# Head of a decoder block: two adaLN vectors summed by TensorE in one-column products instead of by VectorE

## What is computed

```python
mod = jax.nn.silu(c) @ w_ada[layer] + b_ada[layer]
sh_a, sc_a, gt_a, sh_f, sc_f, gt_f = jnp.split(mod, N_MOD, axis=-1)
h = modulate(rms_norm(x, g_attn[layer]), sh_a, sc_a)   # norm * (1 + sc_a) + sh_a
proj = h @ w_in[layer]
```

## Time and profile before

| what | value |
|---|---|
| median of 3 runs | 626.9 us (625.57 to 629.08) |
| the profiled execution | 627.78 us, span of its instructions 625.8 us |
| around the span | 2.0 us |
| TensorE busy | 546.5 us (87%) |
| VectorE busy | 294.6 us (47%) |
| ScalarE busy | 184.0 us (29%) |
| GpSimd busy | 79.0 us (13%) |
| chain that ended last | TensorE 61%, VectorE 13%, DMA 13%, SyncE's queue 7% |

### The profile page before, as it was taken

The page is one execution under the profiler, slowest core; times in us unless marked ns, Lnnn a source line. Parts: engine busy times, 40 slices in busy tenths (PEclk is TensorE's granted clock), DMA queues, the critical chain, the costliest instruction groups (busy, mean ns, idle before and its releaser), DMA issues.

```text
span 625.8 us, 7694 instructions
## 1 busy us (share of the span) xinstructions
PE 546.5 (87%) x2982; PEld 343.9 (55%) x2982; DVE 294.6 (47%) x497; ACT 184.0 (29%) x328; POOL 79.0 (13%) x100
## 2 busy tenths in 40 slices
PE   1499999999978999999999747899999889879797
PEld 1377768778766676665446414445555444434443
DVE  4978673376798636562032284323322222312216
ACT  5265462344444457882042211000000000000002
POOL 8131100000010000000031111111221111110000
PEclk9999999999998999999999958999999999989999
DMA  8986855595262064001930485999999999999957
GB/s 336 398 262 232 308 193 205 172 366 202 68 214 90 2 264 206 1 1 51 426 128 34 186 339 177 407 417 421 422 420 419 419 421 420 421 420 420 410 233 293
DMA packets 42626, 169.28 MB, mean 271 GB/s; under 512 B 7848, under 2 KB 9896, under 8 KB 30308
## 3 DMA queue, kind: packets, MB, share of 16 engines
q1 hardware_dynamic: 32356, 140.81, 56.3%
q0 software_dynamic: 9104, 25.95, 11.8%
q10 hardware_dynamic: 1136, 2.11, 0.9%
HBM read 160.74 MB, written 16.25 MB: 283 GB/s over the span
## 4 chain that ended last, share of the span: by engine, by line
PE 61%; DVE 13%; DMA 13%; SPq 7%; ACT 4%; issue 2%; POOL 0%; DVEq 0%; ACTq 0%; POOLq 0%
PE banks L1784 11%; PE banks L1675 9%; PE banks L1804 5%; DMA qkT<-in_w_dram 5%; DMA obuf<-in_w_dram 4%; PE banks L1627 4%; PE banks L1510 4%; PE banks L1512 4%; PE banks L1511 4%; DVE mixT L893 3%; PE banks L1611 2%; DMA qkT<-in_w_ada_dram 2%; PE banks L1504 2%; PE banks L1502 2%; PE banks L1503 2%
## 5 line engine op out<-in xcount | busy, mean ns | idle before, releaser
L1804 PE MATMUL banks<-stage,work 128*64 128x512 f32 x168 | 60.1, 610 | 6.4 <-ACT work L855 6.4
L853 ACT ACTIVATE work<-banks 128x256 f32<-128x256 f32 x16 | 6.1, 383 | 200.3 <-PE banks L1784 200.3
L1784 PE MATMUL banks<-qkT,work 128*64 128x256 f32 x272 | 62.4, 386 | 0.0
L1675 PE MATMUL banks<-stage,mixT 128*128 128x512 f32 x128 | 56.2, 595 | 0.0
L1324 DVE TENSOR_TENSOR work<-banks,gates 128x1024 f32<-128x1024 f32 x15 | 18.4, 1225 | 74.5 <-PE banks L1804 74.5
L1318 DVE TENSOR_TENSOR work<-work,banks 128x256 f32<-128x256 f32 x16 | 6.7, 421 | 87.6 <-ACT work L853 87.6
L1784 PE MATMUL banks<-hT,work 128*64 128x256 f32 x192 | 44.0, 387 | 2.5 <-DMA qkT<-in_w_dram 2.5
L1512 PE MATMUL banks<-hT_hi,w_lo 128*128 128x512 f32 x112 | 43.8, 391 | 0.0
L893 DVE SCALAR_TENSOR_TENSOR mixT<-stage,small,mixT 128x1024 f32<-128x1024 f32 x32 | 41.0, 1282 | 0.7
L1510 PE MATMUL banks<-hT_hi,w_hi 128*128 128x512 f32 x96 | 40.4, 421 | 0.0
L1675 PEld LDWEIGHTS banks<-stage,mixT 128*128 128x128 f32 x128 | 24.1, 191 | 28.8 <-issue 28.8
(11 more groups left out here) (301 smaller groups left out, 1172.6 us busy)
## 6 DMA issues: line engine op xcount, KB each, us to landing
stage<-in_w_dram SPq DMA_DIRECT2D x31, 1024.0 KB
qkT<-in_w_dram SPq DMA_DIRECT2D x23, 1024.0 KB
stage<-in_w_ada_dram POOLq DMA_DIRECT2D x16, 1024.0 KB, 5.7
hT<-in_w_dram SPq DMA_DIRECT2D x12, 1024.0 KB
stage<-in_w_in_dram SPq DMA_DIRECT2D x5, 2048.0 KB, 11.0
val<-in_w_dram SPq DMA_DIRECT2D x10, 1024.0 KB
mixT<-in_w_dram SPq DMA_DIRECT2D x10, 1024.0 KB
alibi<-in_w_dram SPq DMA_DIRECT2D x5, 1024.0 KB
```

What stands on the lines that cost most here:

```text
L1675: ins = mm(banks[:, w % 5, :], mixT[:, k, t * P:(t + 1) * P], wv[:, k % 4, half * 512:(half + 1) * 512], start=(k == 0), stop=(k == KD - 1))
L1784: ins = mm(banks[half * C:(half + 1) * C, 2, up * F:(up + 1) * F], heT[:, r, k * P + half * C:k * P + (half + 1) * C], ws[2 * place + half ...
L1804: ins = mm(banks[half * C:(half + 1) * C, 4 + 2 * r + col, :], geT[:, fc * P + half * C:fc * P + (half + 1) * C], w2s[2 * place + half][:, ...
```

## The change

VectorE's sums of the two vectors go. TensorE takes the raw weights as the stationary operand, in 128 x 128 blocks with a stride of eight elements, and the column `cs[:, r]` as the moving one, and adds up over the eight rows r in PSUM. A quarter has two rows, so it is 16 products (`column_quarter`), and there are eight quarters. Behind each of the first three quarters come the transposes of a tile of `x`, and the last tile is loaded ahead of the last two quarters and transposed ahead of the last one. Eight bf16 products of 256 columns whose result nothing reads (`HEAD_FILLERS`) stand ahead of the last quarter. In the split of `w_in`, ScalarE no longer rounds the second chunk of weights; VectorE does, behind the first part of `hT_hi`.

```diff
             for i in range(4):
+                if i == 2:
+                    x_tile(NT - 1)
                 ada_quarter(scale_w, SCALE_A, i)
-            x_tile(NT - 1)
...
             w_round(0)
-            w_round(1)
...
             dve.wait_ge(silu_c, 1)
-            first_sums(0, shift_w, shift_used)
-            first_sums(1, scale_w, scale_used)
...
             def w_rest(n):
-                raw, hi, lo, _, _ = split_chunk(n)
-                dve.wait_ge(w_hi_ready, n + 1)
+                raw, hi, lo, arrived, value = split_chunk(n)
+                if n == 1:
+                    dve.wait_ge(arrived, value)
+                    v.tensor_copy(hi, raw).then_inc(w_hi_second, 1)
+                    dve.wait_ge(w_hi_second, 1)
+                else:
+                    dve.wait_ge(w_hi_ready, max(n, 1))
                 v.tensor_tensor(lo, raw, hi.bitcast(F32), ALU.subtract).then_inc(w_split, 1)
-            w_rest(0)
             dve.wait_ge(mod_params_in, 32)
-            dve.wait_ge(col_a, 1)
+            dve.wait_ge(scale_used, KD)
...
             dve.wait_ge(mod_a, 1)
-            w_rest(1)
+            w_rest(0)
             for k in range(KD):
                 dve.wait_ge(hT_raw, k + 1)
                 v.tensor_copy(hT_hi[:, k, :], hT[:, k, :]).then_inc(hT_hi_ready, 1)
+                if k == 0:
+                    w_rest(1)
...
-            def column_sums(v, used):
-
-                pe.wait_ge(used, KD)
-                for k in range(KD):
-                    ins = mm(banks[:, 0, 8 * v + k:8 * v + k + 1],
-                             by_col[:, v, k * P:(k + 1) * P], ones[:, 0:1],
-                             start=(v + k == 0), stop=True, skip_group_check=True)
-                return ins
...
+            def column_quarter(v, i):
+
+                w, used = ((shift_w, shift_used), (scale_w, scale_used))[v]
+                pe.wait_ge(first_in[4 * v + i], 16)
+                for r in range(2 * i, 2 * i + 2):
+                    src = w[r // 4][:, r % 4, :].rearrange("p (j k) -> p k j", k=KD)
+                    for k in range(KD):
+                        ins = mm(banks[:, 0, 8 * v + k:8 * v + k + 1], src[:, k, :], cs[:, r:r + 1],
+                                 start=(v + r + k == 0), stop=(r == KD - 1), skip_group_check=True)
+                    ins.then_inc(used, 1)
+
+            pe.wait_ge(silu_c, 1)
+            for i in range(4):
+                column_quarter(0, i)
+                if i < NT - 1:
+                    x_tile_T(i)
+            for i in range(3):
+                column_quarter(1, i)
+            x_tile_T(NT - 1)
+            for n in range(HEAD_FILLERS):
+                mm(banks[:, 0, 256:512], ones_bf[:], ones_bf[:].unsqueeze(1).to_broadcast([P, 2, P]),
+                   start=False, stop=True, skip_group_check=True)
+            column_quarter(1, 3)
             pe.wait_ge(hT_raw, 1)
```

More of the change, by code:

```diff
@@ L48 @@
 FILLERS = 14
+HEAD_FILLERS = 8
 XT_BANK = (2, 3, 4, 5, 6, 7, 1, 2)
@@ L271, in hymba_block @@
         silu_c, shift_used, ada_used = sem("silu_c"), sem("shift_used"), sem("ada_used")
-        col_a, mod_a = sem("col_a"), sem("mod_a")
+        mod_a = sem("mod_a")
         xn_ready, xT_done = sem("xn_ready"), sem("xT_done")
         hT_raw, hT_hi_ready, hT_lo_dve, hT_lo_pool = (sem(n) for n in ("hT_raw", "hT_hi_ready", "hT_lo_dve", "hT_lo_pool"))
-        w_hi_ready, w_split = sem("w_hi_ready"), sem("w_split")
+        w_hi_ready, w_hi_second, w_split = sem("w_hi_ready"), sem("w_hi_second"), sem("w_split")
         job_done = sem("job_done")
@@ L901, in last_by_col @@
                                               in1=turned(sums), op0=ALU.mult, op1=ALU.add)
-            def first_sums(v, w, used):
-                for k in range(KD):
[L906 to L912, removed]
             v.memset(eps, EPS).then_inc(eps_ready, 1)
@@ L1429, in x_T, with x_tile_T @@
                                            xn[:, t, :].rearrange("p (j k) -> p k j", k=KD)[:, k, :], ident)
-            def column_sums(v, used):
-                pe.wait_ge(used, KD)
-                for k in range(KD):
-                    ins = mm(banks[:, 0, 8 * v + k:8 * v + k + 1],
-                             by_col[:, v, k * P:(k + 1) * P], ones[:, 0:1],
-                             start=(v + k == 0), stop=True, skip_group_check=True)
-                return ins
[L1440 to L1443, removed]
+            def x_tile_T(t):
                 pe.wait_ge(xn_ready, t + 1)
```

## The result

| | before | changed |
|---|---|---|
| median of 4 runs | 626.28 us | 666.27 us (664.98 to 666.4) |
| ratio on record | | 1.0631, 95% interval 1.0608 to 1.0654 |
| profiled execution, its span | 627.78, 625.8 us | 666.28, 664.2 us |
| vectors ready, ScalarE released | 36.8 us | 75.0 us |
| end of the first pair's products | 51.6 us | 90.9 us |

The kernel is 40.0 us slower by the medians and 38.5 by the two profiled executions. The head accounts for all of it: at the end of the first pair the changed kernel is 39.3 us behind, and the projection of the attention output starts 38.2 us later (324.2 against 286.0), from where the distance stays within a microsecond until the end.

The account below looks back on a forecast made before the run. VectorE's sums, not loads, were taken to hold the head; TensorE's lower-clock products would replace them. Vectors +33.1 and 1.6 behind give +34.7 on 627.8, or 662.5; 661.6 us for a median, range 646 to 672.

Parts of the forecast that it names:

- The count and the place: Head, TensorE: 128 products, 256 records at two weight loads per product, behind the loads from the first quarter on.
- The order of the loads: Head: loading x's last tile ahead of two quarters costs and gains nothing, since TensorE is behind the loads.
- Stride: Raw-block weight loads on TensorE: stride of eight taken to add nothing; upper bound 11.3 us (44 ns on each of 256 records).
- my 69.3: Head: time in us at which sums up to the vectors end at the lower clock, against 36.25 before, +33.1.
- Strided weight loads are dearer: Rival for TensorE's raw-block products: all 44 ns come on top of every record, 673 us; chance 0.05.
- My sign for it: Profile sign of dearer strided loads: weight loads of the raw-weight product group showing more than 350 ns.
- Which clock: TensorE in the head: lower clock level taken for all eight quarters, deciding between 28 and 55 us of products.
- an early rise: Rival for the head: one quarter at the lower clock, seven at the higher, +6.8 us, 633.7; chance 0.10.
- My two prices for the two levels: Head's sixteen product groups on TensorE: 54.9 us at the lower clock, 28.3 at the higher.
- Behind the vectors: From ScalarE's release to the first pair's end: 1.6 us more, between 1.0 and 2.6, from VectorE's new work and a later clock rise.
- The six `hT_lo` that end the first pair start 1.0 later: VectorE behind the vectors: 2.1 us of new rounding and `w_lo`, of which waiting absorbs 1.1.
- No loss: Rival: TensorE keeps up with the loads at 97 ns a record, 624.6 us at full success; chance 0.05.

Follow-up runs that it names:

- The run at 142 us: Kernel before, with the one-column products of the third and fourth vector reading blocks at a stride of eight: eight products took 3.67 us against 1.77.
- both runs that have this part: The changed kernel, and the kernel before with only the reordered weight split: the first pair ends 15.9 and 16.6 us behind ScalarE's release, against 14.8 before.
- the strided run: Changed kernel with twenty bf16 products of 512 columns ahead of the first quarter, blocks still strided: quarter 7.42 us, vectors at 77.8 us.

## Why the prediction was right, and where it was not

**The count and the place: right.** 256 records on TensorE in a line without gaps, behind the loads from the first quarter on, VectorE idle until the vectors come, the transposes at 1.53 for a set (1.55 written), the fillers at 1.71 (1.7). So the cause that I gave, two full weight loads for every single column, was the right one. The order of the loads cost and gained nothing: the only wait for a load was the first.

**The pace: too low by 9%.** The step was "*Stride*: I take nothing and keep 11.3 as the upper bound". Measured: 7.45 us for a quarter instead of 6.86, 0.59 x 8 = 4.7 us, of the 5.1 by which the vectors were later than my 69.3. (Most of the rest is in the three quarters without transposes between them, 22.8 us together; no run says why.) I had argued from the duration of a weight load, where 189 ns for strided transposes and 192 for unstrided products looked like one ceiling. The run at 142 us shows that the stride has a pace of its own for float32 products, which a load's duration at the lower clock (335 against 334) does not betray. So my rival "Strided weight loads are dearer", at 0.05, came true in part: 19 of its 44 ns a record. My sign for it, loads of more than 350 ns, would have missed it, for they show 335. The measured 666.3 lies just above my own spread of 657 to 666 and within the range because that reaches up for a part of the stride.

**Which clock: the granted level as predicted, but it decided nothing.** I wrote "This decides between 28 and 55 us" and gave an early rise 0.10 at 633.7. That rival rested on contiguous rows. With the blocks as the change reads them, 7.42 us for a quarter begun at 1.00, so the products would have taken about the same time. My two prices for the two levels held only for contiguous blocks. What I said for the lower level, that this kind of work had not raised the clock from 32.66 to 38.8, is borne out more strongly than I knew: it lets a clock that is up fall, with both PE and PEld at 1.00 busy in the window. The Trainium skill (TensorE: Matmul & The Clock Gate, "What's actually happening") ties the level to activity; in these windows it fell although PE and PEld read busy throughout, so by the profile's busy time alone the rule would have misled here.
The same page's section "LDWEIGHTS (loading the stationary operand)" makes the load's time a matter of its column count alone; its formula gives 107 ns for 128, an estimate. The distance between contiguous records at the higher clock comes near it (1.77 / 16 = 111 ns, though the record of the load itself is 192 ns there). The contiguous ones at the lower clock, 3.43 / 16 = 214 ns, and the strided ones at the higher, 3.67 / 16 = 229, do not.

**Behind the vectors: 1.1 to 1.8 where 1.6 was forecast, partly for the wrong reason.** The wrong step is "The six `hT_lo` that end the first pair start 1.0 later". They started no later at all, 5.84 us behind the release as before: I took 2.1 us for the new work and 0.45 for a cast without a wait, and it was 1.9 (76.49 to 78.35) and 0.37 (2.58 / 7). In both runs that have this part TensorE did not wait for them; it was late from its own stop behind the first `hT_hi` and from the lower clock, which I had priced at 0.6. That the sum came out near is in part luck.

**No loss: rightly small.** I had set its point at 97 ns a record. The strided pace is 2.4 times that.

**Profiled against profiled**: 33.1 written for the vectors, 38.2 measured; 1.6 written behind, 1.1 measured; and 0.9 gained back later in the kernel (39.3 at the end of the pair, 38.4 in the spans), which I did not follow further.

## What to carry to other kernels

A product with one moving column costs a whole 128 x 128 weight load, twice in float32, so ask for each sum which operand should be stationary: the same sums took 7.4 us a quarter with the matrix stationary (6.7 contiguous, 3.5 at the higher clock) and 1.9 at the higher clock with the vector stationary. Read a stationary operand contiguously, and take a pace from a row with the same stride and the same kind of instruction: the strided transposes said nothing of the strided products. Before counting on a higher clock, look for a row that shows the very instruction following it.

## What the runs showed of the hardware that I had not expected

- Float32 one-column products whose stationary block has a stride of eight elements run at 0.229 to 0.233 us a record at either clock level; contiguous 0.109 to 0.111 at the higher and 0.209 to 0.214 at the lower; a stride of two 0.116 at the higher. Transposes at a stride of eight follow the clock, seven in 0.84 and 1.53 us.
- The granted clock fell from 1.00 to 0.5 while TensorE's matmuls and weight loads were busy for 1.00 of the window, with products of one column, strided (from 9.72 us on) or contiguous (from 10.23 on, with seven transposes among them).
- The column of the granted clock can't be trusted before its first fall. It reads 1.00 through all of the changed kernel's head, whose transposes run at the lower pace. Among the twenty fillers of the strided run, durations went from 634 to 379 ns near 7.2 us with no change in that column, so durations have to be read before it.
- Thirty-two records with 64 stationary columns on 64 partitions, alternating between the two halves of the array, took 1.10 us, 0.034 each, less than a third of the 0.111 of the contiguous 128-column records at the higher clock.
